# Reordering the end of an output projection on TensorE, taking tile 0's first gather in fp32, and loading three eighths of one weight half sooner

## What is computed

```python
x = x + (g_a * branch_a + g_b * branch_b) @ w_o      # w_o: 1024 x 1024
x = x + moe_ffn(rms_norm(x, g_ffn), w_router, b_router, w_gu, b_gu, w_down, b_down)
...
logits = (xt @ w_router).astype(jnp.float32) + b_router
top_val, top_idx = lax.top_k(logits, TOP_K)          # 4 of 32 experts
gates = jax.nn.softmax(top_val, axis=-1)
# per expert: hgu = xblk @ w_gu[e] + b_gu[e]; clamped SwiGLU; act @ w_down[e] + b_down[e]
```

## Time and profile before

| what | value |
|---|---|
| median of 3 runs | 1100.96 us (1098.55 to 1101.72) |
| the profiled execution, its own time | 1099.74 us |
| its span in the trace | 1098.0 us |
| PE busy | 1056.9 us (96%) |
| DVE busy | 456.8 us (42%) |
| ACT busy | 174.6 us (16%) |
| DMA moved | 433.20 MB, mean 395 GB/s |

### The profile page before, as it was taken

How to read it: one execution, slowest core, us unless ns; L and a number is a source line. 1 busy time by engine, 2 the same in 40 slices (tenths; PEclk the granted TensorE clock), 3 DMA queues, 4 the chain that set the end, 5 groups by cost and what they waited for, 6 DMA issues and landing times.

```text
span 1098.0 us, 17348 instructions
## 1 busy us (share of the span) xinstructions
PE 1056.9 (96%) x7125; PEld 516.0 (47%) x7127; DVE 456.8 (42%) x766; ACT 174.6 (16%) x295; POOL 9.0 (1%) x20
## 2 busy tenths in 40 slices
PE   8999999999999999999999999999999999999995
PEld 8999975444443333344443333333444333343332
DVE  5567667233333333333333333333333333332344
ACT  5345533100000000000000000000000000000012
POOL 1000110000000000000000000000000000000000
PEclk9999999999999999999999999999999999999998
DMA  9872799999999999999999999999999999999993
GB/s 304 280 215 69 306 409 366 429 427 429 427 429 429 429 427 430 427 428 428 430 429 427 429 427 428 429 429 429 428 428 429 427 429 430 429 426 427 429 422 134
DMA packets 52190, 433.20 MB, mean 395 GB/s; under 512 B 4564, under 2 KB 21480, under 8 KB 26137
## 3 DMA queue, kind: packets, MB, share of 16 engines
q1 hardware_dynamic: 50527, 431.04, 94.5%
q10 hardware_dynamic: 1634, 1.74, 0.5%
HBM read 431.62 MB, written 1.39 MB: 394 GB/s over the span
## 4 chain that ended last, share of the span: by engine, by line
PE 57%; DMA 38%; issue 2%; DVE 2%; SPq 1%; POOL 0%; ACT 0%; ACTq 0%; DVEq 0%; POOLq 0%
DMA down_ring<-in_w_down_dram 23%; PE PS L1107 17%; PE PS L1133 15%; DMA gu_ring<-in_w_gu_dram 15%; PE PS L874 9%; PE PS L1043 3%; PE PS L917 2%; PE PS L1086 2%; PE PS L1088 1%; PE PS L1120 1%; PE PS L1118 1%; PE PS L1147 1%; DVE pick_twice L1539 1%; PE PS L825 1%; PE PS L953 1%
## 5 line engine op out<-in xcount | busy, mean ns | idle before, releaser
L1107 PE MATMUL PS<-gu_ring,XgT 128*64 128x512 f32 x2048 | 469.5, 599 | 5.5 <-DMA gu_ring<-in_w_gu_dram 5.2
L1107 PEld LDWEIGHTS PS<-gu_ring,XgT 128*64 128x64 f32 x2048 | 134.7, 136 | 270.1 <-issue 245.6
L1133 PE MATMUL PS<-down_ring,actT 128*64 128x512 f32 x992 | 222.0, 596 | 15.2 <-DMA down_ring<-in_w_down_dram 15.2
L1573 DVE TENSOR_TENSOR Y<-PS,Y 128x1024 f32<-128x1024 f32 (+1 forms) x96 | 117.0, 1220 | 256.9 <-PE PS L1088 256.9
L1133 PEld LDWEIGHTS PS<-down_ring,actT 128*64 128x64 f32 x992 | 67.5, 137 | 144.7 <-issue 117.3
L1604 DVE SCALAR_TENSOR_TENSOR y_low<-PS,slot_gate,y_high 128x512 fp32r<-128x512 f32 x31 | 23.3, 751 | 237.9 <-ACT y_high L776 237.9
L788 ACT ACTIVATE work<-PS 128x512 f32<-128x512 f32 x32 | 19.1, 597 | 462.4 <-PE PS L1107 462.4
L874 PE MATMUL PS<-h_high,win_high 128*128 128x264 f32 (+1 forms) x256 | 71.7, 289 | 0.0
L874 PE MATMUL PS<-h_high,win_low 128*128 128x264 f32 (+1 forms) x256 | 71.1, 287 | 0.0
L874 PE MATMUL PS<-h_low,win_high 128*128 128x264 f32 (+1 forms) x256 | 71.1, 287 | 0.0
L776 ACT ACTIVATE y_high<-PS,slot_gate 128x512 fp32r<-128x512 f32 x31 | 21.3, 688 | 264.6 <-PE PS L1133 264.6
(11 more groups left out here) (231 smaller groups left out, 782.1 us busy)
## 6 DMA issues: line engine op xcount, KB each, us to landing
gu_ring<-in_w_gu_dram SPq DMA_DIRECT2D x119, 2048.0 KB, 28.7
down_ring<-in_w_down_dram SPq DMA_DIRECT2D x62, 2048.0 KB, 22.8
gu_ring<-in_w_gu_dram SPq DMA_DIRECT2D x18, 1024.0 KB, 9.9
gu_ring<-in_w_in_dram SPq DMA_DIRECT2D x16, 1024.0 KB, 9.7
gu_ring<-in_w_down_dram SPq DMA_DIRECT2D x4, 1024.0 KB, 28.1
down_ring<-in_w_pool_up_dram SPq DMA_DIRECT2D x1, 2048.0 KB, 11.8
gu_ring<-in_w_conv_out_dram SPq DMA_DIRECT2D x2, 1024.0 KB, 6.1
down_ring<-in_w_o_dram SPq DMA_DIRECT2D x1, 2048.0 KB, 8.1
```

The lines of the kernel that those rows point to most:

```text
L1107: last = mm(PS[SLOTS * h:SLOTS * h + SLOTS, b, :], XgT[:, k, :], w[:, D * b + HALF * h:D * b + HALF * h + HALF], start=(k == 0), stop=(k = ...
L1133: last = mm(PS[SLOTS * h:SLOTS * h + SLOTS, bank, :], acts[:, f % 4, f // 4, :], weights[:, f, HALF * h:HALF * h + HALF], start=(f == 0), ...
L1573: tt(Y[rows, t, :].rearrange("p (h n) -> p h n", h=2), PS[rows, bank:bank + 2, :], Y[rows, t, :].rearrange("p (h n) -> p h n", h=2), ALU.a ...
```

## The change

The last piece of the output projection, (1, 1), runs its eight low products in one run, and tile 0's logits come behind it. `turn_rows(1, 1)` moves ahead of the first half of tile 1's logits and of tile 0's counts. Its `residual(1, 1)` moves ahead of tile 0's `top_mask` on DVE, and on ACT the root comes before the copy of the turned rows. Tile 0 of the first gather is taken from fp32 Y with a scaled `pick_first`, as tile 1 was; the two products of `keep_third` for tile 0 move behind on DVE. The fills change from 3, 2, 3 to 2, 3. Three of the eight k rows of w_o's half 0, 768 KB, are issued before the wait on the input projection's end, the other five where all eight were.

```diff
--- before.py
+++ after.py
@@ -38,7 +38,8 @@
 NCHUNK = 32
 WARM = (16, 2, 2, 6)
 EW = E + 8 - TOPK
-FILL = (3, 2, 3)
+FILL = (2, 3)
+EARLY_KS = slice(-(-KT * COLS // HALF), KT)
 MARK = -1e38
 GONE = -3e38
 LOGIT_BANKS = (1, 2, 4)
@@ -96,8 +97,8 @@
         ident = sb("ident", [P, P])
         slot_no = sb("slot_no", [P, 2 * SLOTS])
         pick = sb("pick", [P, NT, SLOTS], BF16)
-        pick_first = sb("pick_first", [P, SLOTS])
-        first_scale = sb("first_scale", [P, 1])
+        pick_first = sb("pick_first", [P, 2, SLOTS])
+        first_scale = sb("first_scale", [P, 2])
         pick_twice = sb("pick_twice", [P, NT, 2 * SLOTS])
         XgT = sb("XgT", [P, KT, SLOTS])
         with nc.sbuf_tensor("junk", [P, 2 * NT * P], BF16) as junk, \
@@ -373,10 +374,12 @@
                 if b == 9:
                     sp.dma_start(pool_up, w_pool_up[0].rearrange("(k p) n -> p k n", p=P)).then_inc(up_landed, 16)
 
-            def load_wo(h):
-                sp.dma_start(wo_half[h], w_o[0].rearrange("(k p) n -> p k n", p=P)[:, :, HALF * h:HALF * h + HALF]
+            def load_wo(h, ks=slice(0, KT)):
+                sp.dma_start(wo_half[h][:, ks, :],
+                             w_o[0].rearrange("(k p) n -> p k n", p=P)[:, ks, HALF * h:HALF * h + HALF]
                              ).then_inc(wo_landed[h], 16)
 
+            load_wo(0, EARLY_KS)
             sp.wait_ge(z_done, 28)
             for h in range(2):
                 sp.dma_start(half_of(conv_out, h),
@@ -403,7 +406,7 @@
                              ).then_inc(down_landed[h], 16)
 
 
-            load_wo(0)
+            load_wo(0, slice(0, EARLY_KS.start))
             load_wo(1)
             load_row(1, 1, 0)
             sp.wait_ge(cb_ready, 4)
@@ -647,7 +650,7 @@
 
             def round_wo(h, j):
 
-                act.wait_ge(wo_landed[h], 16)
+                act.wait_ge(wo_landed[h], 32 - 16 * h)
                 nc.scalar.activation(wo_high[h][:, 4 * j:4 * j + 4, :], wo_half[h][:, 4 * j:4 * j + 4, :],
                                      ACT.Copy).then_inc(wo_rounded, 1)
 
@@ -752,8 +755,8 @@
                 next_part(2 + h, 0, h)
             act.wait_ge(resid, 5)
             half_squares(5, 1, 1)
+            half_root(5, 1)
             keep_turned(4, 1, 1)
-            half_root(5, 1)
             act.wait_ge(normed, 6)
             for h in range(2):
                 part(4 + h, 1, h)
@@ -991,7 +994,7 @@
             out_highs(0, 0)
             pe.wait_ge(mixed, 8)
             for h in range(2):
-                pe.wait_ge(wo_landed[h], 16)
+                pe.wait_ge(wo_landed[h], 32 - 16 * h)
             for k in range(KT):
                 for q in range(4):
                     last = mm(PS[32 * q:32 * q + SAMPLE, 4, 0:256], mT_samp[:, k, :],
@@ -1021,21 +1024,20 @@
             turn_rows(0, 1)
             out_highs(1, 1, range(6, 8)).then_inc(wo_high_read[1], 1)
             out_lows(1, 1, range(0, 4)).then_inc(wo_low_read, 1)
+            out_lows(1, 1, range(4, 8))
             pe.wait_ge(x2_kept, 4)
             route_rows(0)
-            out_lows(1, 1, range(4, 8))
+            pe.wait_ge(pick_early, 1)
+            pe.wait_ge(resid, 5)
+            turn_rows(1, 1)
             route_rows(1, range(0, 4))
             pe.wait_ge(mask_ready, 2)
             count(0, ones[:], 2, True, False)
             count(0, below_small[:], 0, False, True).then_inc(ranks, 1)
+            pe.wait_ge(x2_kept, 5)
+            route_rows(1, range(4, 8))
             count(1, ones[:], 2, True, False)
             count(1, ones[:], 0, False, False)
-            pe.wait_ge(pick_early, 1)
-            pe.wait_ge(resid, 5)
-            turn_rows(1, 1)
-            fill(FILL[0])
-            pe.wait_ge(x2_kept, 5)
-            route_rows(1, range(4, 8))
 
             def gather_parts(k, parts, first, final):
                 m, q = divmod(k, 2)
@@ -1045,22 +1047,26 @@
                               pick[:, t, :], start=(first and n == 0), stop=(final and n == len(parts) - 1))
                 return last
 
-            pe.wait_ge(third_part, 4)
+            def gather_rows(t, final):
+                for k in range(KT):
+                    last = mm(PS[:, 5, SLOTS * k:SLOTS * k + SLOTS], by_row(P, t, k), pick_first[:, t, :], start=False,
+                              stop=(final and k == KT - 1))
+                return last
+
+            pe.wait_ge(third_part, 2)
+            for k in range(KT):
+                gather_parts(k, ((6, 2),), k == 0, False)
             pe.wait_ge(pick_early, 2)
-            for k in range(KT):
-                gather_parts(k, ((0, 0), (2, 0), (4, 0), (6, 2)), k == 0, False)
+            gather_rows(0, False)
             pe.wait_ge(mask_ready, 3)
             count(1, below_small[:], 1, False, True).then_inc(ranks, 1)
             for n, t in enumerate(ORDER):
                 last = count(3, ones[:], t, n == 0, n == NT - 1)
             last.then_inc(counted, 1)
+            fill(FILL[0])
+            pe.wait_ge(pick_ready, 1)
+            gather_rows(1, True).then_inc(gathered, 1)
             fill(FILL[1])
-            pe.wait_ge(pick_ready, 1)
-            for k in range(KT):
-                last = mm(PS[:, 5, SLOTS * k:SLOTS * k + SLOTS], by_row(P, 1, k), pick_first[:], start=False,
-                          stop=(k == KT - 1))
-            last.then_inc(gathered, 1)
-            fill(FILL[2])
 
             def turn_gates():
 
@@ -1456,12 +1462,16 @@
                     done()
 
             def first_pick(t, n):
-                v.wait_ge(ranks, n)
                 if t == 2:
+                    v.wait_ge(ranks, n)
                     place(2)
                     return tt(pick[:, 2, :], slot_no[:, 0:SLOTS], table[:, 0, 2:3].to_broadcast([P, SLOTS]), ALU.is_equal)
-                return stt(pick[:, t, :], slot_no[:, 0:SLOTS], PS[:, RANK_BANKS[t], E * t:E * t + 1],
-                           mask_small[:, t, 0:1].to_broadcast([P, SLOTS]), ALU.is_equal, ALU.mult)
+                v.wait_ge(mask_ready, n)
+                tt(first_scale[:, t:t + 1], mask_small[:, t, 0:1], stat[:, 3, t:t + 1], ALU.mult).then_inc(scale_ready, 1)
+                v.wait_ge(scale_ready, n - 1)
+                v.wait_ge(ranks, n)
+                return stt(pick_first[:, t, :], slot_no[:, 0:SLOTS], PS[:, RANK_BANKS[t], E * t:E * t + 1],
+                           first_scale[:, t:t + 1].to_broadcast([P, SLOTS]), ALU.is_equal, ALU.mult)
 
             wo_rest(0, 0)
             wo_rest(0, 1)
@@ -1485,20 +1495,12 @@
             keep_rest(3, 0, 1)
             for h in range(2):
                 keep_third(h, 2, h)
+            residual(1, 1)
             top_mask(1, 0)
-            residual(1, 1)
-            for h in range(2):
-                keep_third(2 + h, 0, h)
-            v.wait_ge(mask_ready, 2)
+            norm(2, 1)
             first_pick(0, 2).then_inc(pick_early, 1)
-            norm(2, 1)
             top_mask(2, 1)
-            v.wait_ge(mask_ready, 3)
-            tt(first_scale[:], mask_small[:, 1, 0:1], stat[:, 3, 1:2], ALU.mult).then_inc(scale_ready, 1)
-            v.wait_ge(scale_ready, 1)
-            v.wait_ge(ranks, 3)
-            stt(pick_first[:], slot_no[:, 0:SLOTS], PS[:, RANK_BANKS[1], E:E + 1],
-                first_scale[:].to_broadcast([P, SLOTS]), ALU.is_equal, ALU.mult).then_inc(pick_ready, 1)
+            first_pick(1, 3).then_inc(pick_ready, 1)
 
             def keep_gathered(count):
                 v.wait_ge(gathered, count)
@@ -1506,9 +1508,11 @@
                    g_ffn_cols.unsqueeze(2).to_broadcast([P, KT, SLOTS]), ALU.mult).then_inc(xg_ready, 1)
 
             tt(ex, logits[:, :, 0:E], sought[:, :, 0:1].to_broadcast([P, NT, E]), ALU.subtract).then_inc(shifted, 1)
+            keep_third(3, 0, 1)
             keep_rest(4, 1, 0)
+            v.wait_ge(third_part, 3)
+            keep_gathered(1)
             keep_rest(5, 1, 1)
-            keep_gathered(1)
             place(0)
             place(1)
 
@@ -1541,6 +1545,7 @@
                    ).then_inc(twice_ready, 1)
 
             make_pick(1)
+            keep_third(2, 0, 0)
             for h in range(2):
                 keep_third(4 + h, 1, h)
             v.wait_ge(exped, 1)
```

## The result

| kernel | median of 22 runs | range | executions of 22 above 1103 us |
|---|---|---|---|
| before | 1100.37 us | 1098.52 to 1102.14 | 0 |
| changed | 1104.64 us | 1098.47 to 1108.42 | 13 |

The ratio is 1.003 with a 95% interval of 1.0016 to 1.0044: slower by about 0.3%, where I had forecast no change and a range up to 1102.3. The executions of the changed kernel are of two kinds. Nine took 1098.47 to 1102.18 us, with a mean granted clock of PE of 0.995 to 0.998; thirteen took 1103.63 to 1108.42 us, with 0.987 to 0.991. The medians of the two kinds are 1100.24 and 1105.81, 5.6 us apart.

What follows compares the result with a forecast made beforehand. The weight stream at full DMA rate bounds the item loop, so item 0's start sets the end. Sum: 1099.74 - 0.2 (item 0 sooner) - 0 (early w_o) = 1099.5 us, 1100.7 on the median's scale; range 1098.2 to 1102.3.

Steps and rivals of the forecast that it cites:

- the three fills that stood ahead of them only covered a wait: Ahead of tile 1's second logits on PE: reordering starts these logits 1.0 us sooner, the removed fills only covering a wait.
- x between -0.2 and 0.5: Main forecast: x is how many us sooner item 0 starts, 0.2 taken; chance 0.58.
- something that I don't see in the rows: Outcomes outside all cases: faster 0.03, slower 0.02, the same 0.95.
- the end follows item 0's start: Item loop: if item 0 starts x us sooner, the weight stream resumes x us sooner, up to about 2.6 us.
- the early bytes are worth nothing: Early piece of w_o, 0.79 MB: lost in the break at 179 us; value taken 0, other bound 1.8 us.
- The dry stretch at 179 us: Break in the weight stream from 179 to 183 us, ahead of the first issue on `gu_used`; predicted to grow by up to 1.8 us.
- rival B: The early bytes of w_o count in full: 1097.7 us, median 1099.0; chance 0.08.
- DVE's wait for the count: Tile 1's rank count stands behind tile 0's fp32 gather: DVE has the mask at 174.2, nearly 1 us before PE can count.
- Rival A: Tile 0's fp32 gather is over by 174.2, so item 0 starts 1.0 us sooner: 1098.7 us, median 1100.0; chance 0.15.

Runs made afterwards that it cites:

- its slower trace: Changed kernel run again with no edit, trace of a slower execution; median 1105.63 us, ratio 1.0026 to the kernel before.
- with three fills: Changed kernel plus three dummy matmuls of 512 columns behind the turning of tile 1's second half; 1100.17 us, ratio 1.0002.
- the bf16 trace with the fall: Changed kernel with tile 0's first gather from three bf16 parts again, new order kept, run a second time; 1099.87 us, ratio 0.9994.
- with the count 1.0 us sooner: Changed kernel with three fills behind the turning and tile 1's rank count moved to the middle of tile 0's fp32 gather; 1102.11 us, ratio 1.0015.
- the short bf16 gather: Changed kernel with tile 0's first gather from three bf16 parts again, new order kept, first run; 1101.71 us, ratio 1.0000.
- w_o in one piece: Changed kernel with w_o's half 0 loaded in one piece at its old place; 1106.22 us, ratio 1.0054.
- one fill: Changed kernel plus one dummy matmul of 512 columns behind the turning of tile 1's second half; 1105.92 us, ratio 1.0027.
- the run with products added at 27 us: Kernel before with nine dummy matmuls of 280 columns among the small transposes at 27 us; 1102.35 us, ratio 1.0007.

## Why the prediction was wrong

The step that failed is this one: "the three fills that stood ahead of them only covered a wait". I counted their removal at nothing, since PE waited there anyway, and asked only what the new order does to the waits. The forecast, "x between -0.2 and 0.5", had no case in which PE itself runs at half speed, and "something that I don't see in the rows" got 0.02 for the slower side. In every row of before the clock stood at 1.00, and I took it as given for a stretch whose instructions the change replaces.

Point by point:

- That the end follows item 0's start holds within some 2 us, not closer. Span less start is 920.1 us in the changed kernel, 919.6 in its slower trace, 918.0 with three fills and 918.9 in the bf16 trace with the fall, against 919.3 before. So a change of 0.2 us in that start could not have been read from the end.
- That the early bytes are worth nothing holds: the ratio of that edit alone is 1.0001. Where they are lost was half right. The dip stands in the window at 135 us, and most of them are gone by 143 us. The dry stretch at 179 us did not grow, and by the prediction's own sign ("if the dry stretch does not grow, B") that would have meant rival B, which the ratio excludes. The sign was wrong.
- The times of PE, DVE and ACT up to item 0 hold to 0.1 us where the clock is kept, DVE's wait for the count among them. One link was sized wrong: from tile 1's count to its gather took 175.62 - 175.09 = 0.53 us, where I carried over 0.71, and the chain goes through PE's fill there and not through DVE. The 1.9 us of the fp32 gather measured 1.91, so the trace and not the Trainium skill's 107 ns per load (TensorE: Matmul & The Clock Gate, section LDWEIGHTS) gave the right size.
- Rival A did not come, since its condition was not met: tile 0's gather ended at 175.09, not by 174.2. The reason against it, 1.9 us of products, was right. But the prediction had them hold item 0 through DVE's wait for the count, and with the count 1.0 us sooner item 0 started only 0.09 sooner. They hold it on PE itself: with the short bf16 gather item 0 started at 177.95, close to A's 177.7.
- The removal of fills and the change of order were each counted at nothing beyond their waits. Together they brought the slower kind in 20 of 34 executions. In the one trace of that kind of the changed kernel that is 3.9 us ahead of item 0 and 0.3 in its first product run; in the traces with w_o in one piece and with one fill the latter is 1.71 and 1.75 us. On the median of the 22 runs it is 4.3 us.

What causes the fall is shown in part. Two or three fills ahead of tile 1's logits take it away (0 of 11 and 0 of 12), so what PE does there decides. It takes the new order: without these fills the old order has none of the slower kind (0 of 12). It does not take the fp32 gather, since the clock falls ahead of it and falls with the bf16 gather too; that gather makes the fall dearer, because both fp32 gathers run at half clock. Whether it makes it more frequent is open, since the mean clock does not separate the shorter fall of the bf16 kernel from others. The single run of eight low products may have a share (3 of 12 alone, without a trace of it), but undoing it alone did not help. Which of turning, residual and logits in the new order makes the rest is open, and so is why one execution falls and the next one of the same kernel does not.

## What to carry to other kernels

Dummy matmuls that seem only to fill a wait may be holding the clock. Where a change, as this one, takes large products (here the fills) out of a row of small ones, add a case at half clock: the PE time of that stretch once more, with a chance of its own. Look at single executions and their granted clock, not at one profile: the profiled one here showed nearly all steps right and missed the whole loss.

The 0.79 MB loaded ahead were worth nothing here (ratio 1.0001), since the queue ran empty on gates later on, at 134 us first. Before moving bytes ahead, find every later place where the queue runs dry; here most of them were lost at the first.

## What the runs showed of the hardware

The clock fell while PE was busy: 1.97 of 2.00 us from 172 to 174, with small products of 32 columns, transposes and no gap in the chain above 0.1 us.

The Trainium skill (TensorE: Matmul & The Clock Gate, section HAM oscillation) explains falls by long idle gaps of PE. No such gap stands ahead of this one, so that section does not account for it.

A fall also stands at 30 us, at or just behind a row of small transposes, in 11 of the 18 traces. Four of them are of the kernel before with an edit; the one trace of the kernel before itself has none. All four traces of the slower kind have both falls, but neither needs the other: the bf16 trace has the late one alone, seven traces have the early one and not the late. In the slower trace of the changed kernel:

```profile
31.00:32.00 1.00, 1.00 (x8) 1.00 (x7) 0.53 (x1) 0.00 (x0) 0.00 (x0) 0.71 1.10 348
32.00:34.00 2.00, 2.00 (x10) 2.00 (x10) 0.00 (x0) 0.00 (x0) 0.00 (x0) 0.50 1.10 349
34.00:35.00 1.00, 1.00 (x7) 1.00 (x6) 0.00 (x0) 0.00 (x0) 0.00 (x0) 0.58 1.03 325
```

Some 3 us at half clock cost 1.5 us here. In the traces without this fall the last low products start at 166.8 to 167.4 us, in the eight with some 3 us of it at 168.1 to 169.1, and in two with 7 us of it at 170.0 and 170.2 (the run with products added at 27 us is left out). Traces with this early fall alone have a mean clock of 0.993 to 0.996, those with neither fall 0.996 or 0.997. The trace with the products added at 27 us has 0.992 and a third fall near 1035 us, behind a wait of PE. In the 128 executions of the kernel before, the median time falls with the mean clock: 1104.15 us at 0.993 (5 executions), 1102.34 at 0.994, 1101.12 at 0.995, 1100.21 at 0.996, 1098.98 at 0.997 (24). Only the four at 0.998 leave the row, with 1100.63. So much of its spread, which I had taken for noise, goes with the clock. That the early fall makes all of it was not tested.
